# Second expert rows and the choices of the last tiles, set on other picks of one instruction order

## The chip, the cores and the metric

The kernel runs on one core of one Trainium2 chip. The metric is the device time of one execution in microseconds (us); three executions of the kernel before were timed, and a further one was profiled.

## The reference

One step of a decoder layer for 1024 prompt tokens and 64 sample tokens, all in float32, width 1024. The last part, an expert layer, is what the change is about:

```python
h = x + mixed @ w_out                        # mixed: gated pooling mixer and attention
q = (hn @ w_query).reshape(C, 8, 2, 128)     # hn = rmsnorm(h)
s = einsum('chpd,hpnd->chpn', q, sub_keys)   # 8 heads, two halves, 128 sub-keys each
s1, i1 = top_k(s[:, :, 0], 16); s2, i2 = top_k(s[:, :, 1], 16)
idx = the 16 best of the 16 x 16 sums, as i1 * 128 + i2
a = gelu(einsum('cd,chkd->chk', hn, peer_u[idx]))
out = h + einsum('chk,chkd->cd', softmax(top) * a, peer_v[idx])
```

So each token takes 8 x 16 = 128 rows of `peer_u` (a first row, for a dot product) and the same 128 rows of `peer_v` (a second row, for a weighted sum). Each table has 16384 rows of 4 KB.

## The kernel before, in words

**Tiles and groups.** Tokens lie in nine tiles of 128 (tile 4 has the 64 sample tokens). Three groups of tiles, [0, 1], [2, 3, 4] and [5 to 8], go one after the other through the dense part: projections (PE, L1339), pooling, attention, gates (L1585 and L1603), output and query projections (L1631). `lay_out(g)` sets the steps of a group in slots, and `choose(t)` those of a choice, which is the top-k of one tile on DVE (`top_a`, `top_b`, `fin_a`, `fin_b`, L2316 to L2385). The first tile of each group has its choice inside `lay_out`.

**Picks.** A pick n gathers one first row for each of 128 tokens: one indirect DMA of POOL's queue (L975) moves 128 rows of 4 KB, 512 KB, into `ubuf`, and DVE makes the dots (L2401). There are 1088 picks, tile after tile. For all tiles but 3 and 5 a second row is gathered too (L987, also 512 KB, into `vbuf`), 832 in all. It is weighted and added either on DVE (L2422, into `acc`) or on PE as a product with a diagonal matrix (L1717, two matmuls into `pY`, with the matrix made on ACT, L1997). Both buffers are rings of eight.

**Dense pass.** The second rows of tiles 3 and 5 are not gathered. Between picks 712 and 1086 the whole of `peer_v` streams through (128 transfers of 512 KB on SP's queue), DVE builds one-hot matrices (L2459 and L2462), PE turns them into weight matrices (L1674) and multiplies (L1690). During picks 708 to 774 and 904 to 959 the dots read their second operand in PSUM (`pb`) instead of SBUF (`hnf`).

**The order.** Every engine runs one fixed list. `program` goes over the picks n, and behind each pick's own work come the slots that are due at n:

```python
for n in range(NPK + LAG + 5):
    picks(n)
    for slot in DUE.get(n, ()):
        run_slot(stages, slot)
```

`spread(slots, n0, n1)` puts a group's or a choice's slots on the picks from n0 to n1, in proportion to estimated weights. `GROUP_AT` and `CHOOSE_AT` hold these n0 and n1. `TAKEN[n // 32]` says how many second rows are taken in each stretch of 32 picks, and `OWN` how many of these DVE weighs itself; the rest are PE's. A loop makes `VAT` from it (which second rows at which pick), at most two at a pick and not before pick m + 6 for row m. So these tables set the place of POOL's issues and of DVE's and PE's weighing in their lists.

Of the kernel before, what the change touches and what calls it, by code (L numbers as in the profile page):

```python
# [22 lines left out]
def build(nc, x_prompt, x_sample, cache_k, cache_v, cache_logf, state_pool, page_table, norm_mix_g, w_in,  # L23
# [135 lines left out]
    def tile_of(n):  # L159
        return [t for t in range(NT + 1) if START[t] <= n < ENDS[t]][0]  # L160
# [286 lines left out]
    def choose(t):  # L447


        slots = [[("q_load", (t, 0)), ("q_load", (t, 1))], [(x, (t, 0)) for x in CHOICE[0]]]  # L450
        for e in range(PH):
            slots.append([("top_a", (t, e))])
            if e % 2 and e + 1 < PH:
                slots[-1].append(("q_load", (t, e + 1)))
            slots.append([("top_b", (t, e))])
            if e + 1 < PH:
                slots[-1] += [(x, (t, e + 1)) for x in CHOICE[0]]
            if e % 2:
                if e + 2 < PH:
                    slots[-1].append(("q_load", (t, e + 2)))  # L460
                slots.append([("fin_a", (t, e - 1, 2)), ("gexp", (t, e - 1)), ("gexp", (t, e))])
                slots.append([("fin_b", (t, e - 1, 2))])
        return slots
# [85 lines left out]
    def spread(slots, n0, n1):  # L549
        weights = []  # L550
        for slot in slots:
            pe = sum(cost(*x)[0] for x in slot)
            dve = sum(cost(*x)[1] for x in slot)
            weights.append(0.6 + max(pe + 0.6, dve + 0.8))
        total, run = sum(weights), 0.0
        for slot, wt in zip(slots, weights):
            DUE.setdefault(n0 + int((n1 - n0) * run / total), []).append(slot)
            run += wt

    GROUP_AT = [(0, 53), (50, 280), (281, 597)]  # L560
    CHOOSE_AT = {1: (52, 108), 3: (282, 364), 4: (410, 492), 6: (602, 690), 7: (730, 824), 8: (852, 940)}
    ALONE = []
    for g in range(GN):
        slots, ready = lay_out(g)
        if g == 0:
            ALONE = slots[:ready]
            spread(slots[ready:], 0, GROUP_AT[0][1])
        else:
            spread(slots, *GROUP_AT[g])
    for t in CHOOSE_AT:  # L570
        spread(choose(t), *CHOOSE_AT[t])
    for ps in range(len(PASSES)):
# [35 lines left out]

    NI, WIN = 4, 32
    NV = len(VPICK)  # L610
    TAKEN = [18, 15, 15, 14, 10, 8, 10, 12, 34, 30, 32, 35, 29, 27, 33, 17, 21, 19, 32, 16, 16, 4, 18, 37, 32, 32, 32, 40, 26, 34, 36, 28, 30, 32, 8]
    OWN = [0, 0, 3, 9, 10, 8, 10, 10, 4, 15, 16, 7, 28, 16, 19, 15, 20, 13, 9, 0, 0, 1, 2, 0, 6, 16, 23, 7, 0, 0, 10, 8, 13, 15, 3]
    assert sum(TAKEN) >= NV
    last_slot = {}
    for t in GATHERED:
# [8 lines left out]
    for n in range(NPK + LAG):  # L624
        target += TAKEN[n // WIN] / WIN
        while v < NV and len(VAT.get(n, [])) < 2 and VPICK[v] + LAG <= n and (v + 0.5 < target or latest[v] <= n):
            k = VPICK[v] - START[tile_of(VPICK[v])]
            owed += OWN[n // WIN] / max(1, TAKEN[n // WIN])
            on_dve = k < 4 or (k > 4 and owed >= 0.5)
# [1899 lines left out]
```

## Time and profile before

| | |
|---|---|
| median of 3 executions | 3563.71 us (3558.7 to 3564.55) |
| the profiled execution, its own time | 3595.53 us |
| its span | 3593.7 us, 32980 instructions |
| busy, share of the span | PE 86%, DVE 73%, POOL 63%, ACT 26% |
| DMA | 1261.64 MB, of which 1006.76 MB by POOL's gathers |

The first pick's gather is issued at 286 us. The page's busy times don't add up to the span, because the engines work side by side; a stage is read by its stretch. The views by stretch used here have the cuts at the start of the gather of every 32nd pick, so each answers to one number of `TAKEN`.

### The profile page before, as it was taken

Reading aid. Unit: us, or ns where it says so; the run is one execution under the profiler, and the core shown is the slowest. Engines: PE = TensorE matmul, PEld = TensorE weight load, DVE = VectorE, ACT = ScalarE, POOL = GpSimd, SP = SyncE. Lnnn points to the kernel's source line nnn. Section 1 sums busy time; section 2 is a strip of 40 time slices with the busy share of each in tenths; the row PEclk is TensorE's granted clock in tenths of the full one; section 3 lists DMA queues with packets and bytes.
Section 4 is the critical chain, followed back from the end, with each engine's and each line's share of the span. In section 5 each row is a group of like instructions: output and inputs, shape, how many; then the busy total and the mean of one; then the engine's idle time right before and its main releaser. Section 6 shows DMA issues by size and latency. Waiting matters only on the chain.

```text
span 3593.7 us, 32980 instructions
## 1 busy us (share of the span) xinstructions
PE 3075.8 (86%) x9090; PEld 1560.4 (43%) x9090; DVE 2613.4 (73%) x6266; ACT 936.7 (26%) x2287; POOL 2260.8 (63%) x1942
## 2 busy tenths in 40 slices
PE   7897697899987998978998896539998899999987
PEld 4665344467654443333443431115543344544433
DVE  2217877797678888777888898878976768864555
ACT  2112232432123331153331221115510014520000
POOL 0006643577557666878886677776677766677774
PEclk9898898767998998988998998769999899999999
DMA  6359986899999999998999999999999999999999
GB/s 153 99 157 371 363 286 219 284 379 370 372 336 383 370 388 330 329 369 315 383 385 406 400 398 379 357 371 348 351 409 409 409 408 409 369 372 409 409 409 378
DMA packets 426300, 1261.64 MB, mean 351 GB/s; under 512 B 61063, under 2 KB 106791, under 8 KB 426106
## 3 DMA queue, kind: packets, MB, share of 16 engines
q0 software_dynamic: 276480, 1006.76, 73.3%
q1 hardware_dynamic: 141701, 247.01, 20.3%
q10 hardware_dynamic: 7936, 5.77, 0.5%
q8 instruction: 74, 1.21, 0.1%
q14 instruction: 109, 0.89, 0.1%
HBM read 1230.09 MB, written 29.29 MB: 350 GB/s over the span
## 4 chain that ended last, share of the span: by engine, by line
PE 48%; DMA 15%; POOL 12%; DVE 11%; issue 9%; ACT 3%; another core or an unknown queue 2%; SPq 0%; ACTq 0%; DVEq 0%; POOLq 0%
PE pY L1717 13%; DMA vbuf<-in_peer_v_dram,idx 8%; PE pb L1585 8%; POOL ubuf L975 7%; PE pb L1690 5%; POOL vbuf L987 5%; PE pb L1339 4%; DVE ubuf L2401 4%; PE pb L1674 3%; PE pb L1603 3%; PE pb L1631 2%; DMA ubuf<-in_peer_u_dram,idx 2%; DVE acc L2422 1%; PE pb L1442 1%
## 5 line engine op out<-in xcount | busy, mean ns | idle before, releaser
L975 POOL DMA_INDIRECT ubuf<-in_peer_u_dram,idx x1088 | 1275.8, 1173 | 902.2 <-issue 301.4
L2401 DVE CUSTOM_DVE_ANT_0 ubuf<-ubuf,hnf 128x1024 f32<-128x1024 f32 x967 | 1168.6, 1221 | 316.1 <-DMA ubuf<-in_peer_u_dram,idx 292.5
L1717 PE MATMUL pY<-vbuf,dg 128*128 128x512 f32 (+1 forms) x2064 | 1058.7, 644 | 279.3 <-DMA vbuf<-in_peer_v_dram,idx 139.4
L987 POOL DMA_INDIRECT vbuf<-in_peer_v_dram,idx x832 | 981.9, 1180 | 413.2 <-issue 234.9
L1717 PEld LDWEIGHTS pY<-vbuf,dg 128*128 128x128 f32 (+1 forms) x2064 | 376.5, 195 | 772.0 <-issue 539.1
L1690 PE MATMUL pb<-R 128*128 128x512 f32 x1024 | 461.9, 596 | 0.0
L2422 DVE SCALAR_TENSOR_TENSOR acc<-vbuf,gw,acc 128x1024 f32<-128x1024 f32 x316 | 405.4, 1283 | 58.7 <-DMA vbuf<-in_peer_v_dram,idx 46.9
L1585 PE MATMUL pb<-R 128*128 128x256 f32 (+2 forms) x1152 | 361.1, 474 | 5.0 <-DMA R<-in_w_in_dram 3.8
L1987 ACT ACTIVATE gel<-dots 128x4 f32<-128x4 f32 x272 | 55.4, 204 | 1023.9 <-DVE dots L2401 842.0
L1690 PEld LDWEIGHTS pb<-R 128*128 128x128 f32 x1024 | 195.7, 192 | 245.4 <-issue 245.4
L1585 PEld LDWEIGHTS pb<-R 128*128 128x128 f32 x1152 | 221.7, 193 | 142.0 <-issue 94.8
L1997 ACT ACTIVATE dg<-ident,gw 128x128 f32<-128x128 f32 (+1 forms) x516 | 189.4, 384 | 350.3 <-DVE gw L2408 251.7
L1631 PE MATMUL pb<-R 128*128 128x256 f32 (+2 forms) x768 | 249.5, 480 | 5.5 <-DMA R<-in_w_query_dram 4.7
L1339 PE MATMUL pb<-R 128*128 128x512 f32 (+1 forms) x432 | 195.3, 600 | 9.4 <-DVE R L2042 9.4
L1631 PEld LDWEIGHTS pb<-R 128*128 128x128 f32 x768 | 148.1, 196 | 97.2 <-issue 68.2
L1674 PEld LDWEIGHTS pb<-R 128*128 128x128 f32 x1024 | 130.9, 194 | 97.4 <-ACT R L1958 50.7
L1674 PE MATMUL pb<-R 128*128 128x64 f32 x1024 | 136.9, 278 | 25.1 <-ACT R L1958 21.8
L2401 DVE CUSTOM_DVE_ANT_0 ubuf<-ubuf,pb 128x1024 f32<-128x1024 f32 x121 | 146.7, 1213 | 8.1 <-DMA ubuf<-in_peer_u_dram,idx 6.7
L1603 PE MATMUL pb<-R 128*128 128x512 f32 (+1 forms) x288 | 129.3, 610 | 10.4 <-DVE R L2285 10.4
L1987 ACT ACT_TABLE_LOAD x107 | 137.3, 1283 | 2.5 <-issue 0.5
L1958 ACT ACTIVATE R<-R 128x64 f32<-128x64 f32 x512 | 134.6, 336 | 10.3 <-DVE R L2462 7.5
L1339 PEld LDWEIGHTS pb<-R 128*128 128x128 f32 (+1 forms) x432 | 78.3, 186 | 105.7 <-issue 95.5
(260 smaller groups left out, 2749.7 us busy)
## 6 DMA issues: line engine op xcount, KB each, us to landing
R<-in_peer_v_dram SPq DMA_DIRECT2D x128, 512.0 KB
R<-in_w_in_dram SPq DMA_DIRECT2D x12, 2048.0 KB
R<-in_w_in_dram SPq DMA_DIRECT2D x24, 1024.0 KB
R<-in_w_query_dram SPq DMA_DIRECT2D x24, 1024.0 KB
ubuf<-in_peer_u_dram,idx POOLq DMA_INDIRECT x1088
vbuf<-in_peer_v_dram,idx POOLq DMA_INDIRECT x832
R<-in_w_out_dram SPq DMA_DIRECT2D x12, 1024.0 KB
R<-in_x_prompt_dram SPq DMA_DIRECT2D x16, 512.0 KB, 9.0
```

What stands on the lines that cost most here:

```text
L975: pool.indirect_dma_start(out=ubuf[:, n % RING, :], out_offset=None, in_=peer_u[0], in_offset=bass.IndirectOffsetOnAxis(ap=idx[:, t % NI, ...
L987: pool.indirect_dma_start(out=vbuf[:, v % RING, :], out_offset=None, in_=peer_v[0], in_offset=bass.IndirectOffsetOnAxis(ap=idx[:, t % NI, ...
L1339: ins = pe.matmul(pb[0:rows, 2 + o % 3, :], xnT(g)[:, c, cols(i)], wr[j % 2][:, c, :], start=(c == 0), stop=(c == KD - 1))
L1585: ins = pe.matmul(pb[:, out % 5, 0:N], w_four(x)[:, d % NG, kk * P:(kk + 1) * P], rhs, start=(d == 0), stop=(d == last))
L1603: ins = pe.matmul(pb[0:rows, b0 + half, :], mixedT(g)[:, c, cols(i)], w_rows(12 + c // 2)[:, c % 2, half * 512:(half + 1) * 512], start=(c ...
L1631: ins = pe.matmul(pb[:, 2 * (e % 2) + c, 0:N_[g]], w_cols(x)[:, d, c * P:(c + 1) * P], hnT(g)[:, d, :], start=(d == 0), stop=(d == KD - 1))
L1674: ins = pe.matmul(pb[:, 4, c:c + NB], oh_a[o % OHR][:, a, :], oh_b[o % OHR][:, a, :], start=True, stop=True)
L1690: ins = pe.matmul(pb[:, 2 * j + c, :], dw[j][:, b % NB, :], vr[u % VRR][:, c * 512:(c + 1) * 512], start=(b % NB == 0), stop=(b % NB == NB ...
L1717: ins = pe.matmul(pY[0:rows, half, :], dg[:, CPE[m] % RDG, 0:rows], vbuf[:, v % RING, half * 512:(half + 1) * 512], start=first, stop=(t ! ...
L1987: act.activation(gel[:, q % 2, :], dots[:, q % 2, :], ACT.Gelu).then_inc(gel_d, 1)
L2401: dve.tensor_tensor_reduce(ubuf[:, n % RING, :], ubuf[:, n % RING, :], hn, 1.0, 0.0, ALU.mult, ALU.add, dots[:, q % 2, n % GRP:n % GRP + 1 ...
L2422: dve.scalar_tensor_tensor(a, vbuf[:, v % RING, :], gw[:, t % NI, k:k + 1], a, ALU.mult, ALU.add).then_inc(v_dve, 1)
```

## The change

Only four tables of numbers change:

```diff
--- before.py
+++ after.py
@@ -557,8 +557,8 @@
             DUE.setdefault(n0 + int((n1 - n0) * run / total), []).append(slot)
             run += wt
 
-    GROUP_AT = [(0, 53), (50, 280), (281, 597)]
-    CHOOSE_AT = {1: (52, 108), 3: (282, 364), 4: (410, 492), 6: (602, 690), 7: (730, 824), 8: (852, 940)}
+    GROUP_AT = [(0, 50), (50, 280), (281, 600)]
+    CHOOSE_AT = {1: (52, 108), 3: (282, 364), 4: (416, 492), 6: (602, 690), 7: (718, 836), 8: (840, 940)}
     ALONE = []
     for g in range(GN):
         slots, ready = lay_out(g)
@@ -608,8 +608,8 @@
 
     NI, WIN = 4, 32
     NV = len(VPICK)
-    TAKEN = [18, 15, 15, 14, 10, 8, 10, 12, 34, 30, 32, 35, 29, 27, 33, 17, 21, 19, 32, 16, 16, 4, 18, 37, 32, 32, 32, 40, 26, 34, 36, 28, 30, 32, 8]
-    OWN = [0, 0, 3, 9, 10, 8, 10, 10, 4, 15, 16, 7, 28, 16, 19, 15, 20, 13, 9, 0, 0, 1, 2, 0, 6, 16, 23, 7, 0, 0, 10, 8, 13, 15, 3]
+    TAKEN = [18, 15, 15, 14, 14, 4, 22, 8, 34, 30, 42, 33, 21, 35, 29, 13, 13, 19, 28, 16, 16, 8, 18, 37, 22, 32, 32, 50, 26, 30, 36, 28, 30, 24, 20]
+    OWN = [0, 0, 3, 9, 14, 4, 22, 6, 4, 15, 21, 7, 21, 20, 18, 13, 13, 15, 8, 0, 0, 2, 2, 0, 4, 16, 23, 8, 0, 0, 10, 8, 13, 8, 7]
     assert sum(TAKEN) >= NV
     last_slot = {}
     for t in GATHERED:
```

As the loop lays them out, the second rows by stretch are (all others stay as they are, and so do those from pick 704 on, except that single rows there move between DVE and PE):

| picks | before: rows (DVE + PE) | now |
|---|---|---|
| 128 to 160 | 10 (10 + 0) | 14 (14 + 0) |
| 160 to 192 | 8 (8 + 0) | 4 (4 + 0) |
| 192 to 224 | 10 (10 + 0) | 22 (22 + 0) |
| 224 to 256 | 12 (10 + 2) | 8 (6 + 2) |
| 320 to 352 | 32 (16 + 16) | 42 (21 + 21) |
| 352 to 384 | 35 (7 + 28) | 33 (7 + 26) |
| 384 to 416 | 29 (27 + 2) | 21 (20 + 1) |
| 416 to 448 | 27 (17 + 10) | 35 (21 + 14) |
| 448 to 480 | 33 (19 + 14) | 29 (18 + 11) |
| 480 to 512 | 17 (15 + 2) | 13 (13 + 0) |
| 512 to 544 | 21 (20 + 1) | 13 (13 + 0) |
| 544 to 576 | 19 (13 + 6) | 19 (15 + 4) |
| 576 to 608 | 32 (9 + 23) | 28 (8 + 20) |
| 672 to 704 | 4 (1 + 3) | 8 (2 + 6) |

Up to pick 384 that is 249 rows, was 233; from 384 to 640 it is 174, was 194. In all 832 remain, 313 of them on DVE (was 316). Group 0's rest now ends at pick 50 (was 53) and group 2 at 600 (was 597). Tile 4's choice lies on picks 416 to 492 (was 410 to 492), tile 7's on 718 to 836 (was 730 to 824), tile 8's on 840 to 940 (was 852 to 940).

**DVE at picks 204 and 205**, inside the gates of group 1 (L2283 and L2285 are merges of the gates, L2408 the weights of four picks). Before:

```order
L2401 ISA ubuf,dots<-ubuf,hnf 128x1024
L2401 ISA dots 128x1
L2283 TENSOR_TENSOR R<-R,pb 128x320
L2285 TENSOR_TENSOR R<-R 128x320
L2401 ISA ubuf,dots<-ubuf,hnf 128x1024
L2401 ISA dots 128x1
L2408 TENSOR_TENSOR gw<-gel,gw 128x4
L2283 TENSOR_TENSOR R<-R,pb 128x320
L2285 TENSOR_TENSOR R<-R 128x320
L2283 TENSOR_TENSOR R<-R,pb 128x320
L2285 TENSOR_TENSOR R<-R 128x320
```

Now:

```order
L2401 ISA ubuf,dots<-ubuf,hnf 128x1024
L2401 ISA dots 128x1
L2422 SCALAR_TENSOR_TENSOR acc<-vbuf,gw,acc 128x1024
L2283 TENSOR_TENSOR R<-R,pb 128x320
L2285 TENSOR_TENSOR R<-R 128x320
L2401 ISA ubuf,dots<-ubuf,hnf 128x1024
L2401 ISA dots 128x1
L2408 TENSOR_TENSOR gw<-gel,gw 128x4
L2422 SCALAR_TENSOR_TENSOR acc<-vbuf,gw,acc 128x1024
L2283 TENSOR_TENSOR R<-R,pb 128x320
L2285 TENSOR_TENSOR R<-R 128x320
L2283 TENSOR_TENSOR R<-R,pb 128x320
```

Behind the dot of pick 204, and again behind that of pick 205, now stands a second row on DVE (L2422), ahead of the merges.

**DVE at picks 393 to 397**, in group 2's attention. Before:

```order
L2422 SCALAR_TENSOR_TENSOR acc<-vbuf,gw,acc 128x1024
L2401 ISA ubuf,dots<-ubuf,hnf 128x1024
L2401 ISA dots 128x1
L2422 SCALAR_TENSOR_TENSOR acc<-vbuf,gw,acc 128x1024
L2401 ISA ubuf,dots<-ubuf,hnf 128x1024
L2401 ISA dots 128x1
L2422 SCALAR_TENSOR_TENSOR acc<-vbuf,gw,acc 128x1024
L2401 ISA ubuf,dots<-ubuf,hnf 128x1024
L2401 ISA dots 128x1
L2422 SCALAR_TENSOR_TENSOR acc<-vbuf,gw,acc 128x1024
L2401 ISA ubuf,dots<-ubuf,hnf 128x1024
L2401 ISA dots 128x1
```

Now:

```order
L2422 SCALAR_TENSOR_TENSOR acc<-vbuf,gw,acc 128x1024
L2401 ISA ubuf,dots<-ubuf,hnf 128x1024
L2401 ISA dots 128x1
L2401 ISA ubuf,dots<-ubuf,hnf 128x1024
L2401 ISA dots 128x1
L2422 SCALAR_TENSOR_TENSOR acc<-vbuf,gw,acc 128x1024
L2434 TENSOR_TENSOR acc<-pY,acc 128x1024
L2401 ISA ubuf,dots<-ubuf,hnf 128x1024
L2401 ISA dots 128x1
L2422 SCALAR_TENSOR_TENSOR acc<-vbuf,gw,acc 128x1024
L2401 ISA ubuf,dots<-ubuf,hnf 128x1024
L2401 ISA dots 128x1
```

Before, a dot and a second row take turns; now some dots have no second row behind them, and the end of tile 1 (L2434, an addition that reads PSUM) comes between.

**Runs of DVE.** A run is here an unbroken row, in DVE's list, of operations that read two full rows in SBUF: dots on `hnf` and second rows (L2422), with at most the small L2408 between them. Operations of runs beyond their third number 52 before and 58 now on picks 128 to 256, 118 and 97 on picks 384 to 512, 27 and 36 on picks 512 to 544.

**DVE at picks 742 and 743**, among the one-hot matrices of the dense pass (L2459, L2462). Before:

```order
L2401 ISA ubuf,dots<-ubuf,pb 128x1024
L2401 ISA dots 128x1
L2459 TENSOR_TENSOR R<-iota,R 128x512
L2462 TENSOR_TENSOR R<-iota,R 128x256
L2401 ISA ubuf,dots<-ubuf,pb 128x1024
L2401 ISA dots 128x1
L2335 TENSOR_TENSOR eq<-v 128x64
L2335 TENSOR_TENSOR eq<-v 128x48
L2339 MAX top_s<-eq 128x8
L2340 MAX_INDEX top_p<-top_s,eq 128x8
```

Now:

```order
L2401 ISA ubuf,dots<-ubuf,pb 128x1024
L2401 ISA dots 128x1
L2459 TENSOR_TENSOR R<-iota,R 128x512
L2462 TENSOR_TENSOR R<-iota,R 128x256
L2401 ISA ubuf,dots<-ubuf,pb 128x1024
L2401 ISA dots 128x1
L2459 TENSOR_TENSOR R<-iota,R 128x512
L2462 TENSOR_TENSOR R<-iota,R 128x256
```

Tile 7's choice had a step here (L2335 to L2343, its `top_b`); on its longer stretch no step is due at pick 743.

## Rows read from the trace of the kernel before

**Rows 1.** The page: busy time of each engine; DMA in 40 slices, in tenths.

```profile
PE 3075.8 (86%) x9090; PEld 1560.4 (43%) x9090; DVE 2613.4 (73%) x6266; ACT 936.7 (26%) x2287; POOL 2260.8 (63%) x1942
...
DMA  6359986899999999998999999999999999999999
```

**Rows 2.** Busy time by stretches of 32 picks, a late one: us, engines, PEclk, DMA share, GB/s.

```profile
3254.70:3352.20 97.50, 97.50 (x228) 42.94 (x227) 48.56 (x75) 8.10 (x27) 69.26 (x65) 1.00 1.03 409
```

**Rows 3.** The same view, picks 384 to 544 and 576 to 608.

```profile
1493.60:1590.50 96.90, 75.56 (x189) 29.20 (x188) 76.55 (x109) 40.25 (x64) 78.29 (x62) 0.88 0.95 343
1590.50:1701.70 111.20, 87.37 (x219) 35.85 (x218) 85.39 (x212) 44.85 (x81) 90.09 (x60) 0.83 0.90 326
1701.70:1805.30 103.60, 101.38 (x241) 44.60 (x241) 87.92 (x199) 31.16 (x55) 83.78 (x66) 1.00 1.02 381
1805.30:1882.20 76.90, 76.90 (x183) 34.02 (x182) 67.86 (x137) 26.62 (x37) 61.98 (x49) 1.00 1.00 381
1882.20:1972.60 90.40, 72.92 (x169) 33.27 (x168) 72.84 (x111) 16.39 (x29) 60.27 (x54) 0.87 1.02 406
...
2067.60:2167.20 99.60, 90.15 (x217) 35.40 (x216) 95.92 (x305) 27.99 (x62) 72.52 (x64) 0.97 1.03 395
```

**Rows 4.** Instructions of POOL between 1493 and 1883 us, grouped by line.

```profile
L975 POOL DMA_INDIRECT ubuf<-in_peer_u_dram,idx x129 | 174.9, 1356 | 42.5 <-issue 39.0 <-DVE dots L2401 3.4
L987 POOL DMA_INDIRECT vbuf<-in_peer_v_dram,idx x107 | 141.8, 1325 | 32.6 <-issue 31.7 <-PE pY L1717 0.9
```

**Rows 5.** Timeline of POOL, then of DVE, at the longest gather issue.

```profile
1505.89 10.48 POOL L987 DMA_INDIRECT vbuf<-in_peer_v_dram,idx  x1 [0.30 <-issue]
1516.67 0.93 POOL L975 DMA_INDIRECT ubuf<-in_peer_u_dram,idx  x1 [0.31 <-issue]
...
1514.34 1.21 DVE L2401 CUSTOM_DVE_ANT_0 ubuf<-ubuf,hnf 128x1024 f32<-128x1024 f32 x1
```

**Rows 6.** Busy time by stretches of 32 picks: picks 128 to 256, then 320 to 384.

```profile
692.00:778.90 86.90, 79.42 (x382) 51.99 (x379) 79.12 (x161) 27.66 (x48) 60.15 (x43) 0.76 1.01 378
778.90:857.10 78.20, 76.13 (x337) 58.11 (x337) 67.03 (x138) 17.91 (x31) 65.42 (x40) 0.63 1.00 371
857.10:942.70 85.60, 83.38 (x303) 57.97 (x303) 53.60 (x92) 23.57 (x33) 51.27 (x43) 0.98 1.01 370
942.70:1055.10 112.40, 100.26 (x310) 56.70 (x309) 76.71 (x159) 23.58 (x44) 55.58 (x45) 0.94 0.95 355
...
1266.50:1377.50 111.00, 105.54 (x264) 45.52 (x263) 94.07 (x223) 35.09 (x71) 73.12 (x65) 0.98 1.00 368
1377.50:1493.60 116.10, 99.68 (x261) 45.82 (x261) 98.10 (x214) 14.59 (x47) 80.45 (x68) 0.90 0.99 345
```

**Rows 7.** The page: dots and second rows, on DVE and on PE.

```profile
L2401 DVE CUSTOM_DVE_ANT_0 ubuf<-ubuf,hnf 128x1024 f32<-128x1024 f32 x967 | 1168.6, 1221 | 316.1 <-DMA ubuf<-in_peer_u_dram,idx 292.5
...
L1717 PE MATMUL pY<-vbuf,dg 128*128 128x512 f32 (+1 forms) x2064 | 1058.7, 644 | 279.3 <-DMA vbuf<-in_peer_v_dram,idx 139.4
...
L2422 DVE SCALAR_TENSOR_TENSOR acc<-vbuf,gw,acc 128x1024 f32<-128x1024 f32 x316 | 405.4, 1283 | 58.7 <-DMA vbuf<-in_peer_v_dram,idx 46.9
```

**Rows 8.** Busy time by stretches of 32 picks: picks 672 to 704, then 736 to 768.

```profile
2307.60:2361.80 54.20, 13.07 (x20) 3.35 (x20) 51.39 (x132) 5.81 (x18) 40.01 (x36) 0.59 0.94 346
...
2449.60:2547.50 97.90, 88.39 (x405) 53.81 (x404) 86.04 (x230) 56.41 (x199) 64.74 (x65) 1.00 0.96 351
```

**Rows 9.** Instructions of DVE between 2449 and 2548 us, by line.

```profile
L2401 DVE CUSTOM_DVE_ANT_0 ubuf<-ubuf,pb 128x1024 f32<-128x1024 f32 x32 | 38.8, 1212 | 0.0
L2459 DVE TENSOR_TENSOR R<-iota,R 128x512 f32<-128x512 f32 x34 | 23.3, 686 | 5.9 <-PE pb L1674 2.7 <-remote 2.4 <-issue 0.6
L2462 DVE TENSOR_TENSOR R<-iota,R 128x256 f32<-128x256 f32 x34 | 14.4, 423 | 0.0
```

**Rows 10.** Waits of POOL, then of DVE, between 857 and 943 us.

```profile
POOL ubuf L975 <- DVE dots L2401: 22.4, 7, 6.7
...
DVE R L2281 <- PE pb L1585: 16.1, 7, 7.0
```

## Prediction of the time after the change

> **What bounds the kernel now.** The page first: no engine is busy throughout, PE has 86% of the span, DVE 73%, POOL 63%, but the DMA line stands at 9 from the seventh slice nearly to the end [rows 1]. So I went on to the busy times by stretches of 32 picks. A late one shows what a full DMA looks like: share 1.03 at 409 GB/s [rows 2]. A gathered row of 512 KB, 524288 bytes, then costs 1.28 us. I take 1.03 as full, and for a stretch of T us call T x (1.03 - share) / 1.03 its DMA room.
>
> The second thing to see is in the stretches from pick 384 to 512 [rows 3]. The share falls to 0.95 and 0.90, yet PE and DVE are not full. POOL is: between 1493 and 1883 us its 129 + 107 = 236 gathers take 174.9 + 141.8 = 316.7 us, and 42.5 + 32.6 = 75.1 us lie between them, 0.3 us of issue each but for about 4 us [rows 4]. Together that is the whole stage. A plain issue takes 0.93 us and 0.31 us before it [rows 5], so 1.24 us per row, close to the DMA's own 1.28. Over 0.94 us each, the 236 issues spend 316.7 - 221.8 = 94.9 us too much. The worst takes 10.48 us, and through it DVE runs dots and second rows without a pause; the last of these is a dot from 1514.34 us on, and it is 0.8 us after that dot's end that POOL is through [rows 5]. I read it as POOL held up by DVE's runs.
>
> A rule of the Trainium skill speaks on this, "SBUF — State Buffer", section Who interferes with whom: a DVE instruction with two SBUF inputs contends only with a GpSimd instruction that reads SBUF, and a lock lasts for one instruction. By that alone a gather would lose one dot's time at most, and the trace doesn't agree: 10.48 us is eight of them.
>
> **The change, part by part.** Nothing is added or removed but a place: 832 second rows before and after. What a row costs is what bounds its new place, and what it gives is what bounded its old one.
>
> *Rows added, picks 128 to 384* (16 more) [rows 6]. On picks 128 to 160, 4 more: 5.1 us of DMA, less room of 86.9 x 0.02 / 1.03 = 1.7, is +3.4. On 160 to 192, 4 fewer, but PE is busy 76.1 of 78.2 us and the rows are DVE's, so only 2.1 of 5.1 us comes out: -2.1. On 192 to 224, 12 more, all weighed on DVE: 15.4 less room of 1.7 is +13.7. DVE carries it: 53.6 + 12 x 1.283 [rows 7] = 69.0 us in a stretch that is then 99.3. On 224 to 256, 4 fewer where share is 0.95 and something else leads (at its best 5.1): I take -2.0, nearer nothing, since PE is busy 100.3 of 112.4. On 320 to 352, 10 more: 12.8 less room of 3.2 is +9.6; PE's 105.5 gets 5 rows of two matmuls of 0.644 us [rows 7], 112.0, which is below the new 120.6. On 352 to 384, 2 fewer, PE's: -1.3, half of what DMA or PE would give. Sum: +21.3. Bounds: the 26 added rows at the full 1.28 and nothing given back by the 10 removed, +33; the added ones as here and the removed ones at 1.28, 3.4 + 13.7 + 9.6 - 12.8 = +13.9.
>
> *Rows removed, picks 384 to 640* (20 fewer) [rows 3]. On 384 to 416, 8 fewer issues of 1.24 give -9.9, and on 416 to 448, 8 more take them back, +9.9, since POOL leads in both. On 448 to 480, 4 fewer: -5.0. On 480 to 512, 4 fewer, but PE is busy all of the 76.9 us and loses 2 rows, 2.6 us; between 2.6 and 5.0 I take -4.0. On 512 to 544, 8 fewer with the DMA at 1.02: -10.3. On 576 to 608, 4 fewer, where DVE is at 95.9 of 99.6 and gets rid of a single row, 1.3 us: between 1.3 and 5.1 I take -3.2. Sum: -22.5. Bounds: all 20 rows at 1.28, -26; where PE, DVE or half a row's price decides (3.9 and 2.6 by PE's rows, 5, 1.3), -13.
>
> *The four rows on picks 672 to 704* find DMA room of 54.2 x 0.09 / 1.03 = 4.7 for their 5.1 us, PE nearly idle, and DVE at 51.4 of 54.2, which takes one row more [rows 8]. +1.0, bounds 0 and +5.
>
> *POOL's long issues.* 97 operations stand beyond the third of DVE's runs on picks 384 to 512, was 118, and 133 instead of 145 with the next stretch: 8% to 18% fewer. Of the 94.9 us [rows 4] that would be 8 to 17 us; but many issues are a little long in every stage, and the later start of tile 4's choice packs DVE tighter from pick 416 on. I take -5, bounds +5 and -15. (By the skill's rule, named above, this term is 0 and the sum 5 us less of a gain.)
>
> *Longer choices of tiles 7 and 8.* On picks 736 to 768 DVE is busy 86.0 us of 97.9, and waits most of the rest; the DMA has room for 97.9 x 0.07 / 1.03 = 6.7 us [rows 8]. Of the 86.0, dots are 38.8 and one-hot matrices 23.3 + 14.4 [rows 9]; some 8 us are left for the choice, and at 118 picks instead of 94 a fifth of that goes, 1.7 us. Tile 8's brings about as much or less further on. Together -3, bounds 0 and -8 (room of 6.7 and a bit). Work brought forward to picks 718 to 730 meets a DVE with time to spare. The ends of groups 0 and 2, moved by 3 picks, and single rows that change between DVE and PE after pick 704, where the DMA leads [rows 2], I cost at nothing: at 409 GB/s the transfers hide them; were that cover gone, three rows at 1.283 us are 4 us at most.
>
> **Sum.** 21.3 - 22.5 + 1.0 - 5.0 - 3.0 = -8.2 us. The profiled execution took 3595.5 us, so it would be 3587.3; the median of the timed ones is 3563.7, 0.9% lower, and I carry the difference over as it is: **3555.5 us**.
>
> **The rivals.**
> 1. *A mere exchange.* If POOL's long issues stay as they are and the later stages don't move, then rows cost what they save: 21.3 - 22.5 + 1.0 = -0.2, and with half of the choices' gain -1.7, so 3562 us. For it: row prices of 1.24 and 1.28 are nearly one. Against it: the 94.9 us. It is also where the skill's rule leads. Chance 0.22.
> 2. *The long issues mostly go.* They need a full run of DVE, and the alternation of dot and second row on picks 384 to 416 is what the plan thins out most (27 to 20 on DVE). If 20 of the 94.9 us go in place of 5, it ends at -23, 3540 us. Against it: 21 of the rows of the next stretch are DVE's, was 17. Chance 0.17.
> 3. *PE's clock falls under the gates.* This is the one on the slow side. On picks 192 to 224 PE works 83.4 of 85.6 us at a granted clock of 0.98, and DVE waits 16.1 us for its gates [rows 6, 10]. With 12 more rows the stretch gets 99.3 us long, PE waits for merges that DVE does after a late dot, and a PE with gaps has had 0.76 and 0.63 just ahead, 0.83 to 0.88 on picks 384 to 448 [rows 3, 6]. At 0.98 x 83.4 / 99.3 = 0.82 it becomes the bound; at 0.75 the stretch takes 109 us, +10, and picks 320 to 352 (PE 112 of 120.6) get the same, some +5. With POOL's relief gone besides, which the added runs on picks 192 to 224 can undo, it's -8.2 + 10 + 5 + 3 = +10, so 3574 us. Against it: PE's gates are fed by four buffers ahead, and POOL waits 22.4 us for dots there [rows 10], so it is not short of time. Chance 0.21.
>
> That the plan doesn't do what it says is no rival: the loop's counts are in the table above, and all gathers keep their distance of six picks.
>
> **The numbers.** The forecast has 0.40, its own range is -2 to -15 (all bounds at once would be -35 to +30, which is not likely, since the terms are apart). A measurement of this kernel can tell some 0.2%, 7 us, from no change, so of the 0.40 I put 0.28 on faster and 0.12 on the same. Rival 1: 0.03 faster, 0.17 the same, 0.02 slower. Rival 2: all 0.17 faster. Rival 3: 0.02 the same, 0.19 slower. Sum: 0.48, 0.31, 0.21. The range reaches from 3532, rival 2 and a stronger relief, to 3577, rival 3 and a little more.
>
> **What would show it.** Picks 128 to 384 should take 21 us longer (801.6 us before, from 692.0 to 1493.6), picks 384 to 640 some 27 us less (740.9 before, 1493.6 to 2234.5), picks 736 to 768 between 1 and 6 less. The clock on picks 192 to 224 should stay above 0.9; below 0.82, rival 3 is right. POOL's issues on picks 384 to 512 should have fewer above 3 us; as many as before speak for rival 1. The forecast is wrong if the first part grows by more than 30 us, or if the stages after pick 704, which I count at -3, move by more than 8 either way.

## The result and the profile after

| | before | the change |
|---|---|---|
| median of 7 executions | 3564.18 us | 3532.89 us |
| ratio, 95% interval | | 0.9918 [0.9898, 0.9939] |
| profiled execution, its span | 3593.7 us | 3525.3 us |

The change makes the kernel 0.8% faster, 31 us of the medians. The forecast was 3555.5, that is 8 us faster, so the gain is nearly four times what was forecast; the result is at the lower edge of the range, 0.9 us inside it. The two profiled executions differ by 68 us, over twice that. Picks 704 to 960 alone account for 28 us of it (793.3 and 765.7 us), and the experiments show that these are no part of the change.

The page's lines that answer to [rows 1]:

```profile
PE 3075.5 (87%) x9102; PEld 1566.2 (44%) x9102; DVE 2608.8 (74%) x6263; ACT 931.3 (26%) x2285; POOL 2245.0 (64%) x1942
...
DMA  6349986799999999999999999999999999999999
```

The busy times hardly move (PE 3075.5, DVE 2608.8, POOL 2245.0 us): the work is the same, and what goes is idle time.

Busy time by stretches of 32 picks, in the columns of [rows 2], for picks 128 to 256 and 320 to 384, as in [rows 6]:

```profile
687.40:775.30 87.90, 81.56 (x370) 55.48 (x369) 82.79 (x163) 27.00 (x46) 66.42 (x47) 0.73 1.04 397
775.30:851.60 76.30, 75.20 (x348) 57.81 (x346) 62.21 (x132) 19.62 (x33) 54.81 (x36) 0.66 0.99 356
851.60:941.80 90.20, 85.47 (x304) 59.15 (x305) 66.03 (x107) 23.57 (x33) 64.90 (x55) 0.96 1.03 401
941.80:1053.50 111.70, 100.44 (x308) 56.19 (x307) 74.27 (x155) 23.63 (x44) 50.90 (x40) 0.94 0.95 355
...
1257.90:1390.40 132.50, 120.41 (x301) 52.26 (x299) 108.82 (x249) 37.59 (x77) 83.44 (x74) 0.97 0.99 368
1390.40:1490.00 99.60, 91.27 (x240) 42.19 (x241) 89.39 (x191) 13.25 (x42) 79.77 (x66) 0.95 1.03 375
```

Picks 192 to 224 grew from 85.6 to 90.2 us with 12 rows more, at 401 GB/s, was 370, and PE's clock was 0.96, before 0.98. Picks 320 to 352 took 132.5 us, was 111.0, but the next 32 took 99.6, was 116.1. The cuts lie at POOL's issues, and POOL moves against the others, so these two are read together: 232.1 us, was 227.1, with 8 rows more.

The same view for picks 384 to 544, as in [rows 3]:

```profile
1490.00:1575.80 85.80, 68.47 (x187) 27.97 (x186) 63.47 (x101) 38.59 (x63) 69.64 (x54) 0.90 0.97 351
1575.80:1685.10 109.30, 88.97 (x221) 36.19 (x220) 91.70 (x209) 45.68 (x83) 88.88 (x67) 0.86 0.98 354
1685.10:1781.30 96.20, 94.84 (x229) 41.73 (x228) 84.09 (x200) 31.01 (x53) 77.57 (x62) 1.00 1.03 396
1781.30:1857.00 75.70, 75.70 (x180) 33.52 (x179) 71.48 (x148) 21.13 (x32) 57.81 (x46) 1.00 0.99 374
1857.00:1934.70 77.70, 69.27 (x163) 31.52 (x162) 64.94 (x103) 13.65 (x28) 53.35 (x46) 0.93 1.02 406
```

Together 444.7 us, was 479.0. POOL's gathers on picks 384 to 512, to be held against [rows 4]:

```profile
L975 POOL DMA_INDIRECT ubuf<-in_peer_u_dram,idx x129 | 172.1, 1334 | 43.5 <-issue 38.1 <-DVE dots L2401 5.4
L987 POOL DMA_INDIRECT vbuf<-in_peer_v_dram,idx x98 | 122.8, 1253 | 29.9 <-issue 29.6 <-PE pY L1717 0.3
```

There are 227 issues in 367 us; over 0.94 us each they spend 294.9 - 213.4 = 81.5 us, was 94.9 for 236. Issues of over 3 us on picks 384 to 512 number 9 now and 8 before.

### The profile page after: what moved, and what is told of

Read it like the earlier page. It is cut to its first block, busy times and chain, and to the rows that moved or that the text cites. A ratio compares the mean times of both kernels' runs of the same rounds, so it can differ in the third digit from the quotient of the medians.

```text
span 3525.3 us, 32998 instructions
## 1 busy us (share of the span) xinstructions
PE 3075.5 (87%) x9102; PEld 1566.2 (44%) x9102; DVE 2608.8 (74%) x6263; ACT 931.3 (26%) x2285; POOL 2245.0 (64%) x1942
## 4 chain that ended last, share of the span: by engine, by line
PE 46%; DMA 15%; POOL 11%; DVE 9%; issue 6%; SPq 2%; ACT 2%; ACTq 0%; DVEq 0%; POOLq 0%
PE pY L1717 15%; DMA vbuf<-in_peer_v_dram,idx 8%; POOL ubuf L975 7%; PE pb L1690 7%; PE pb L1585 6%; POOL vbuf L987 5%; PE pb L1339 3%; PE pb L1603 3%; DVE ubuf L2401 3%; PE pb L1674 3%; PE pb L1631 2%; DMA ubuf<-in_peer_u_dram,idx 2%; PE pb L1442 1%; PE pb L1558 1%; DVE acc L2422 1%
## 5 line engine op out<-in xcount | busy, mean ns | idle before, releaser
L1717 PE MATMUL pY<-vbuf,dg 128*128 128x512 f32 (+1 forms) x2076 | 1058.1, 641 | 226.5 <-DMA vbuf<-in_peer_v_dram,idx 152.4
L987 POOL DMA_INDIRECT vbuf<-in_peer_v_dram,idx x832 | 964.2, 1159 | 390.4 <-issue 202.2
L1717 PEld LDWEIGHTS pY<-vbuf,dg 128*128 128x128 f32 (+1 forms) x2076 | 379.4, 195 | 719.9 <-issue 470.5
L2422 DVE SCALAR_TENSOR_TENSOR acc<-vbuf,gw,acc 128x1024 f32<-128x1024 f32 x313 | 401.8, 1284 | 45.2 <-DMA vbuf<-in_peer_v_dram,idx 41.3
L1987 ACT ACTIVATE gel<-dots 128x4 f32<-128x4 f32 x272 | 55.4, 204 | 988.3 <-DVE dots L2401 987.1
L1339 PE MATMUL pb<-R 128*128 128x512 f32 (+1 forms) x432 | 195.7, 599 | 11.1 <-DVE R L2042 11.1
```

What stands on the lines that cost most here:

```text
L987: pool.indirect_dma_start(out=vbuf[:, v % RING, :], out_offset=None, in_=peer_v[0], in_offset=bass.IndirectOffsetOnAxis(ap=idx[:, t % NI, ...
L1339: ins = pe.matmul(pb[0:rows, 2 + o % 3, :], xnT(g)[:, c, cols(i)], wr[j % 2][:, c, :], start=(c == 0), stop=(c == KD - 1))
L1717: ins = pe.matmul(pY[0:rows, half, :], dg[:, CPE[m] % RDG, 0:rows], vbuf[:, v % RING, half * 512:(half + 1) * 512], start=first, stop=(t ! ...
L1987: act.activation(gel[:, q % 2, :], dots[:, q % 2, :], ACT.Gelu).then_inc(gel_d, 1)
L2422: dve.scalar_tensor_tensor(a, vbuf[:, v % RING, :], gw[:, t % NI, k:k + 1], a, ALU.mult, ALU.add).then_inc(v_dve, 1)
```

## Experiments

There are three sets of four kernels, each set on a chip of its own with the kernel before beside it; ratios are against it on the same chip. The time of a stretch of picks is that of one profiled execution. In the diffs, OWN goes with TAKEN as in the change, unless it is shown.

**The kernel before once more, profiled.** No edit.

> The kernel before, unchanged, profiled once more, to see how far a stretch of 32 picks moves from one profiled execution to the next. The first profile took 3595.5 us where the timed executions took 3564. Theory A (the gain lies in picks 384 to 640): the stretches from pick 704 to 960 come out near 766 us here too, as in the profile of the change, not 793 as in the first profile, so that the 28 us lost there are of that one execution. Theory B (the later stages really gained from the longer choices): 793 us again, within 5. Time between 3555 and 3600 us.

Measured: 3616.4 us on a chip where the kernel before has a median of 3646 in 23 executions. Picks 704 to 960 took 805 us. Neither A's 766 nor B's 793 came out, nor a time between 3555 and 3600, so this chip alone doesn't decide it; the last set does. This one execution is 30 us faster than the median, which is to be kept in mind where its stretches are compared below.

**The plan alone.**

```diff
-    TAKEN = [18, 15, 15, 14, 10, 8, 10, 12, ...
+    TAKEN = [18, 15, 15, 14, 14, 4, 22, 8, ...
-    OWN = [0, 0, 3, 9, 10, 8, 10, 10, ...
+    OWN = [0, 0, 3, 9, 14, 4, 22, 6, ...
```

> The change's TAKEN and OWN alone; the ranges of groups and choices as before. Theory A (the plan of second rows carries the gain): ratio 0.992 to 0.995, some 18 to 30 us faster. Theory B (the choices of tiles 7 and 8 carry it): ratio 0.998 to 1.001. Theory C (half and half): about 0.996. My prediction's terms without those of the choices give -5 us, ratio 0.9985.

Measured: 0.9897 [0.9864, 0.9931]. The plan carries the gain (A, and somewhat beyond it). The stretches 320 to 384, 384 to 448 and 448 to 512 of the kernel before, on that chip:

```profile
1266.30:1496.40 230.10, 206.64 (x524) 91.92 (x523) 192.40 (x436) 49.63 (x118) 153.65 (x131) 0.93 0.98 351
1496.40:1702.50 206.10, 160.08 (x410) 64.56 (x409) 161.88 (x320) 84.71 (x145) 169.49 (x120) 0.86 0.94 338
1702.50:1886.70 184.20, 178.74 (x423) 78.65 (x422) 158.52 (x340) 59.98 (x94) 149.42 (x115) 1.00 1.00 377
```

and with the plan alone:

```profile
1279.10:1502.80 223.70, 209.71 (x533) 92.64 (x532) 196.53 (x440) 49.52 (x117) 157.70 (x140) 0.95 1.03 376
1502.80:1708.80 206.00, 158.80 (x411) 64.21 (x409) 156.12 (x314) 83.68 (x146) 165.78 (x120) 0.88 0.92 332
1708.80:1879.40 170.60, 168.82 (x401) 74.21 (x401) 155.44 (x342) 58.53 (x91) 131.71 (x106) 1.00 1.02 393
```

With 8 rows more, picks 320 to 384 became 6.4 us shorter, at 376 GB/s. With 8 fewer, picks 448 to 512 became 13.6 us shorter. On picks 384 to 448 the number of rows is the same (8 fewer, then 8 more), and so is the time. The whole profiles differ by 9.5 us only (3614.6 and 3605.1), the medians by 39: that of the kernel before was a fast execution.

**The choices of tiles 7 and 8 alone.**

```diff
-    CHOOSE_AT = {... 7: (730, 824), 8: (852, 940)}
+    CHOOSE_AT = {... 7: (718, 836), 8: (840, 940)}
```

> Only the choices of tiles 7 and 8 get their longer ranges (718 to 836 and 840 to 940). Theory A: ratio 0.998 to 1.0 (my term was -3 us, 0.9992). Theory B: 0.992 to 0.995, and picks 704 to 960 are over 15 us shorter in the profile, with the DMA share above 1.0 on picks 736 to 768, was 0.96. Theory C: about 0.996.

Measured: 0.9986 [0.9962, 1.0009], as A had it; the interval holds both my -3 us and nothing. Picks 704 to 960 took 805.5 us, against 805.1 of the kernel before.

**The other ranges alone.**

```diff
-    GROUP_AT = [(0, 53), (50, 280), (281, 597)]
+    GROUP_AT = [(0, 50), (50, 280), (281, 600)]
-    CHOOSE_AT = {... 4: (410, 492) ...}
+    CHOOSE_AT = {... 4: (416, 492) ...}
```

> Only the ends of group 0 (50) and group 2 (600), the start of group 2's and tile 4's choice as in the change (tile 4 on 416 to 492). I costed these at nothing: ratio 0.999 to 1.001. A rival: tile 4's choice, packed tighter, costs up to 5 us by itself (1.0014), or its later start frees POOL on picks 410 to 416 and gains up to 5 (0.9986).

Measured: 0.9959 [0.9934, 0.9984], faster by more than either side expected; nothing was not right. In its profile POOL's excess over 0.94 us on picks 384 to 448 is 42 us, against 56 to 57 in the two profiles of the kernel before, and on picks 448 to 512 it is 44, was 39 and 42. The stretch 384 to 448 took 202.2 us, was 208.1 and 206.1, but the next one, to 512, took 188.1 us, was 180.5 and 184.2, so the two together are as long as before: the profiles don't show where the time of this run was gained.

**The change whole, in the second set.** No edit to the change.

> The change whole, on the chip of this set. If its parts add up as on the last chip (0.9897 x 0.9986 x 0.9959), the ratio is 0.984; if it repeats its own first comparison, 0.992. The stretch from pick 704 to 960 is 766 us in the first profile of the change and 793 to 809 us in all others: if that belongs to the change, it is again under 780 here; if to the chip or to the one execution, it is within 8 us of the other kernels of this set.

Measured: 0.9946 [0.9914, 0.9978]. The parts do not add up to 0.984. Picks 704 to 960 took 811.8 us, as the others of the set (807 to 818), so the short 766 is not the change's.

**The early part of the plan alone.**

```diff
 TAKEN, of the stretches of 32 picks from 128, and of the one from 512:
-10, 8, 10, 12 ... 21
+14, 4, 22, 8 ... 13
```

> The plan changed only on picks 128 to 256 (8 rows more in sum) and 512 to 544 (8 fewer). By my prediction's prices, DMA room taken from the busy share: +13.0 - 10.3 = +3 us, ratio 1.001. Theory R (the room is what is missing to 409 GB/s, some 8 us on picks 192 to 224, so the 8 rows come in for 3 us or less): +3 - 10.3 = -7 us, ratio 0.998, with picks 128 to 256 between 0 and 5 us longer (363 and 358 us before) and picks 512 to 576 some 10 us shorter (185 and 182 us).

Measured: 1.0022 [0.9988, 1.0057]. The time can't tell the two: R's 0.998 is just outside, my ledger's 1.001 well inside. Picks 512 to 576 took 173.5 us, 8 to 12 shorter, as both had it; picks 128 to 256 took 365.5 us, 2 to 8 longer than in the profiles of the kernel before on other chips. On this set's own chip they took 369.4 us in the middle part alone, which has no row added there, so here the 8 rows cost nothing that shows. Part of the time is picks 384 to 448, 218.7 us and thus 10 longer without an edit there; one other profile has that too. Picks 192 to 224 in it, with 22 rows, at 398 GB/s and a clock of 0.98:

```profile
865.50:954.90 89.40, 84.15 (x305) 58.45 (x306) 65.96 (x106) 23.57 (x33) 63.95 (x55) 0.98 1.03 398
```

**The middle part alone.**

```diff
 TAKEN, of the six stretches of 32 picks from 320 on:
-32, 35, 29, 27, 33, 17
+42, 33, 21, 35, 29, 13
```

> The plan changed only on picks 320 to 512: 10 more and 2 fewer up to 384, 8 fewer and 8 more up to 448, 8 fewer up to 512. By my prediction's prices +8.3 - 9.0, and -5 for POOL's long issues: -6 us, ratio 0.998. Theory R (room up to 409 GB/s): +0.4 - 9.0 - 5 = -14 us, ratio 0.996. If the long issues of POOL are no matter: 5 us less gain in both, and the excess of POOL's issues over 0.94 us on picks 384 to 512 stays at 92 us or more.

Measured: 0.9951 [0.9926, 0.9976], -18 us, between -9 and -27. My -6 is outside, R's -14 inside. POOL's excess on picks 384 to 512 stayed at 57 + 35 = 92 us, so its long issues had no part in this, and R's number without them is -9, at the edge of the interval. So the middle part is the greater half of the gain. Picks 320 to 384 with their 8 added rows took 224.4 us, against 228.1 in the early part alone on the same chip, so my +8.3 for them was off.

**Twelve rows more on picks 192 to 224.**

```diff
 the change, and of TAKEN (from 192; from 448 and 480):
-22 ... 29, 13
+34 ... 23, 7
 OWN: 34 ... 15, 7
```

> The change and 12 rows more on picks 192 to 224 (34, all weighed on DVE), taken from picks 448 to 512 (6 and 6). Theory R: the room there is used up by the change's own 12 (share 1.03 at 401 GB/s), so these cost 15 us and bring 15 us: no different from the change, within 4 us. If rows come in free there still (PE or DVE's waits for gates lead): 10 to 15 us faster than the change. If PE's clock falls below 0.82 there, as my slow rival had it: slower than the change by 5 us or more.

Measured: 0.9955 [0.9928, 0.9982], beside 0.9946 of the change: no difference, as R had it, and as 1.28 us a row at either end would have it. The stretch took 104.9 us and PE kept its clock:

```profile
860.60:965.50 104.90, 99.20 (x353) 68.53 (x354) 80.19 (x117) 26.06 (x37) 79.84 (x66) 0.97 1.03 396
```

Picks 128 to 256 grew by 16.6 us against the change on this chip (369.8), picks 448 to 512 shrank by 9.3 (175.9 to 166.6). The slow rival, the clock under the gates, is out: 0.97 with PE at 99.2 of 104.9 us.

**The change and the plan alone, once more, in the third set.**

> The change whole once more, beside the three kernels below on one chip: ratio 0.992 to 0.995, as its first two comparisons (0.9918 and 0.9946).

> TAKEN and OWN alone, a second time (0.9897 on another chip). If the ranges of groups and choices give nothing on top of the plan: the same as the change whole, within 0.003. If they give what they gave alone (0.9959 x 0.9986): 0.005 above the change. Picks 384 to 512 should show POOL's excess over 0.94 us at 53 + 32 us, as in the first profile of this kernel, against 40 to 46 + 36 to 44 us with the new ranges.

Measured: 0.9930 [0.9903, 0.9956] and 0.9946 [0.9927, 0.9965]. On top of the plan the ranges and choices give 0.0016, within the intervals, and less than the 0.0055 that they gave alone. POOL's excess with the plan alone was 54 + 29 us, as expected; with the change 49 + 35, so its first part was not quite down to 46. Picks 736 to 768 of the change here:

```profile
2415.50:2502.00 86.50, 85.32 (x395) 52.41 (x394) 82.08 (x210) 53.47 (x190) 64.62 (x65) 1.00 1.03 408
```

of the plan alone, with the old choices:

```profile
2420.30:2509.20 88.90, 84.74 (x385) 52.38 (x383) 81.20 (x221) 54.28 (x192) 65.58 (x65) 0.98 1.02 401
```

and of the change on the second set's chip:

```profile
2447.30:2550.90 103.60, 94.11 (x407) 57.28 (x406) 86.67 (x221) 56.56 (x201) 66.94 (x64) 0.94 0.93 334
```

The longer choices make 2.4 us here, close to my term. On the first set's chip the same picks took 97.8, 103.1 and 96.8 us with the old choices and 103.0 with the longer ones, so one profile can't carry it. The chip makes 17 us: the share is 1.03 at 408 GB/s on one and 0.93 at 334 on the other, for the same kernel. Picks 704 to 960 took 763 to 765 us in all four kernels of this set, old choices or new.

**Ten rows more on picks 352 to 384.**

```diff
 the change, and of TAKEN (from 352; from 448 and 480):
-33 ... 29, 13
+43 ... 24, 8
```

> The change and 10 rows more on picks 352 to 384 (43), taken from picks 448 to 512 (5 and 5). In the profiles with 8 more rows on picks 320 to 384 these took 228 us, and 230 us without, so the rows came in free. Theory R (free as long as there is room up to 409 GB/s; on picks 352 to 384 of the change's profile 375 GB/s over 99.6 us, room 8.3 us): the 10 rows cost 4 to 5 us and bring 12, so 7 us faster than the change. Theory F (full, as I priced them): 12.8 us for 12, no difference. Theory P (PE leads there, 91 of 100 us, and 7 of these rows are its own, 9 us): slightly slower or equal.

Measured: 0.9976 [0.9957, 0.9996], slower than the change by 0.0046, some 16 us. Picks 320 to 384 and 448 to 512:

```profile
1258.50:1506.10 247.60, 226.34 (x582) 101.56 (x581) 201.32 (x442) 54.85 (x130) 172.68 (x150) 0.96 0.99 367
1712.60:1880.10 167.50, 161.81 (x381) 71.25 (x380) 147.26 (x340) 49.76 (x81) 126.49 (x97) 0.98 1.00 370
```

and of the change on this chip:

```profile
1260.70:1498.10 237.40, 213.28 (x541) 94.79 (x540) 198.25 (x439) 50.73 (x119) 164.25 (x140) 0.94 0.99 362
1696.40:1867.90 171.50, 170.17 (x406) 75.02 (x405) 158.28 (x355) 51.49 (x85) 134.62 (x106) 1.00 1.01 387
```

R's 7 us faster is out, and F's no difference hardly fits; P (PE leads on the new place) had the direction. The ten rows cost 10.2 us on their new place and gave back 4.0 on the old one; picks 384 to 448 between them, without an edit, took 8.2 us longer (206.5, was 198.3). The old place gives no more: PE is busy 170.2 of 171.5 us there in the change already, and 8 of the 10 rows taken out are DVE's. On the new place all ten rows are PE's, and its busy time grew by 13.0 us. The DMA moved 362 GB/s there, which by R's room up to 409 would have taken them in for nothing.

**PE weighs more on picks 384 to 448.**

```diff
 the change, and of OWN (from 384 and 416):
-21, 20
+11, 12
```

> The change, but on picks 384 to 448 DVE weighs 23 of the 56 second rows instead of 41 and PE the 18 others; operations beyond the third of DVE's runs fall there from 65 to 49. Theory A (DVE's runs hold up POOL's issues): POOL's excess on these picks falls from 40 to 46 us to 30 or less, and the stretch from 195 to 206 us to 185 to 195. Theory B (the skill's rule, or anything else makes the long issues): the excess stays at 40 us or more, the stretch is as long or up to 10 us longer, since PE gets 23 us of work more. Theory A is not told apart from B by the time alone, since PE may lead; the excess tells it.

Measured: 1.0004 [0.9987, 1.0021], slower than the change by 26 us. POOL's excess on these picks fell from 49.0 to 35.1 us; in the other profiles with the change's rows there it is 40 to 46. That is the direction of A, but not its number (30 or less), and the stretch got longer by 20 us. It and DVE's longest wait:

```profile
1492.50:1710.90 218.40, 178.89 (x462) 74.62 (x460) 127.36 (x269) 89.70 (x163) 147.71 (x120) 0.91 0.89 320
...
DVE gw L2408 <- ACT gel L1987: 62.5, 12, 13.3
```

In the change:

```profile
1498.10:1696.40 198.30, 158.80 (x406) 64.23 (x404) 153.56 (x300) 84.26 (x146) 161.70 (x120) 0.87 0.98 346
...
DVE gw L2408 <- ACT gel L1987: 20.6, 7, 10.7
```

POOL's lateness went down, but DVE's waits for the gelu on ACT (L1987) went from 20.6 to 62.5 us. ACT makes the diagonal matrices for each row that PE weighs, in one list with the gelu and attention's exponentials. So fewer rows on DVE go with shorter issues of POOL, though a DVE that waits more may do that as well as one with shorter runs; and giving the rows up costs more than it brings. That ACT's list is the way of this loss is read from the waits; no run tested it by itself.

## Why the prediction was right, and where its sizes were wrong

The direction and the place of the gain were right. The range held by 0.9 us only, at its end for a stronger relief of POOL, which is not what happened, so that it held is in part luck; the forecast's ratio, 0.9977, is outside the interval in two of the three comparisons of the change and at the edge of the third. The sizes of the terms, against the stretches of picks in nine profiles, each side by its mean: without the plan (the kernel before twice, and the two kernels with choices or ranges alone) and with it (the change three times, the plan alone twice):

| picks | without | with | difference | predicted |
|---|---|---|---|---|
| 128 to 256 | 359.4 | 365.7 | +6.2 | +13.0 |
| 256 to 320 | 210.8 | 208.6 | -2.2 | 0 |
| 320 to 384 | 230.1 | 229.5 | -0.6 | +8.3 |
| 384 to 448 | 209.0 | 202.8 | -6.2 | 0 |
| 448 to 512 | 182.6 | 171.5 | -11.1 | -9.0 |
| 512 to 576 | 183.9 | 173.2 | -10.7 | -10.3 |
| 576 to 640 | 172.0 | 171.8 | -0.2 | -3.2 |
| sum | | | -24.8 | -1.2 (and -5 for long issues) |

The two sides are not from the same chips: three of the four without come from the first set's, where the kernel before has a median of 3646 us, three of the five with from chips where it has 3564 and 3565. On the first set's chip alone, picks 128 to 384 took 797.8 to 801.5 us without the plan and 800.3 with it. The -6.2 on picks 384 to 448 is not the plan's: on the first set's chip 206.1 us became 206.0 with the plan alone, and the short times (195.2 to 202.2, but also 206.2) are those of kernels with the new ranges.

1. **Rows added: the term that failed.** I had +21.3; the stretches say +3.4 (means of 800.4 and 803.8 us for picks 128 to 384, which spread over 4 and 10 us). The step was the DMA room, which I took from the busy share, 1.03 less the share. At share 1.01 and 370 GB/s that leaves 1.7 us on picks 192 to 224. With 12 rows more the same stretch moved 401 GB/s. Had I taken the room as what is missing to 409 GB/s, it is 85.6 x 39 / 409 = 8.2 us there, and 111.0 x 41 / 409 + 116.1 x 64 / 409 = 29 us on picks 320 to 384. Then 15.4 - 8.2 = +7 and about 0 come out, near the +4.7 and -0.6 of the means. The middle part alone (0.9951, and 224.4 us on picks 320 to 384) is the run that speaks most against my price. So the added rows came in nearly free, and the distance of the share from 1.03 was no measure of the DMA's room. That the rate up to 409 GB/s is the right measure is not shown: it was fitted to these stretches, and with ten rows more on picks 352 to 384 it failed: the room there is 237.4 x 47 / 409 = 27 us, the rows should have been free, and they cost 10.2 us. There PE's added work, 13.0 us, is the nearer price.
   PE's own price was misread as well. `L1717` has 2064 records for 516 rows, so four to a row and not two, and a row takes some 2 us of PE (1058.7 / 516), not 1.29. The 5 rows on picks 320 to 352 would have made 105.5 into about 116, still below the 120.6, so no term that was taken hangs on it but the ends of some bounds. And the DMA line of the page stands at 9 from the ninth slice on, not the seventh.
2. **Rows removed** were right in sum: -22.5, measured -22.0 on picks 448 to 640.
3. **Picks 672 to 704**, +1.0: picks 640 to 704 took 127.2 us without and 128.0 with the plan. Right within their spread.
4. **POOL's long issues**, -5. The excess on picks 384 to 512 went from a mean of 92 to 84 us, but the issues of over 3 us did not get fewer: 7 or 8 of them in the four profiles without, 7 to 9 in the five with. By the prediction's own sign that speaks for rival 1. On picks 384 to 448 it is the ranges that lower the excess: 53 to 57 us in all seven profiles with the old ranges of groups and of tile 4's choice, and 40 to 49 in all six with the new ones and DVE's share of the change or of before. I had expected the later start of that choice to work the other way. On picks 448 to 512 it is 44 us with the ranges alone, 32 to 42 with neither, 32 and 29 with the plan alone. Over both stretches the plan alone has 85 and 83 us, the ranges alone 86, neither 87 to 99. So the size was met without the cause that I gave, and the share of this in the time stays open: the ranges gave 15 us alone, with an interval from 6 to 24, and 6 on top of the plan, within noise.
5. **Choices of tiles 7 and 8**, -3: 0.9986 alone, with an interval that holds nothing too, and 2.4 us on picks 736 to 768 of one chip. Not contradicted; more can't be told.
6. **The rivals.** A mere exchange is out, by 0.9897 and 0.9946 for the plan alone: the rows cost less than they save. Its other half, that the long issues stay, came true. The long issues' going is out as the cause, though its time, 3540 us, is nearer than mine: the middle part gained its 18 us with the excess at 92. The clock under the gates is out, by 0.95 to 0.98 on picks 192 to 224 with 22 rows there, and 0.97 with 34. Of the low clocks that it leaned on, 0.76 and 0.63 were no sign of a PE with gaps: PE was busy 79.4 of 86.9 and 76.1 of 78.2 us there.
7. **The sum** against one profiled execution carried no error of its own, but a comparison of the two profiles would: 28 of their 68 us lie on picks 704 to 960, where two chips differ by 48 us (764 and 812 us for the change). By the sign that the prediction set itself, more than 8 us after pick 704, it would be wrong on these two profiles; on one chip these picks take the same time with the change and with the plan alone (764.3 and 765.3 us), so the sign most likely read chips and not the change. The other sign, more than 30 us on picks 128 to 384, did not come: 0.9 us.

The change whole has been compared three times: 0.9918, 0.9946, 0.9930. No kernel beat it on a chip where both ran; of two that go on in its direction, 12 rows more early made no difference and 10 more in the middle were slower.

## What to carry to other kernels

Before pricing a transfer by a DMA that seems full, look at what it moves, not only at how long it is busy: 370 GB/s at share 1.01 had room for more. But a rate below the best is no promise of room: at 362 GB/s ten rows more cost 10.2 us, where they were all PE's. When rows are shifted from one stage to another, both ends need their own bound, and the gain ends at the first stage where another engine takes over, as PE did on picks 448 to 512. And two profiles of one kernel on two chips can differ by more than a change is worth, so a stage's gain is believed from several.

## What was not expected of the hardware

The change itself had another speed in one stage on another chip: picks 736 to 768 took 86.5 us at 408 GB/s on one and 103.6 us at 334 GB/s on another, where the whole kernel took 3539 and 3617 us (medians).

A gather issue of POOL grows from 0.93 us to 7 to 12 us at its longest, in each of the 14 profiles, and through it DVE has no gap of more than 0.03 us: it runs dots and second rows out of SBUF with small operations between them, in four of the profiles also steps of a choice. Each profile has 12 to 17 issues of over 3 us, and all of them lie before pick 490. The rule of the Trainium skill that the prediction named ("SBUF — State Buffer", Who interferes with whom) has a lock that ends with the instruction; an issue of 10.48 us, held through nine dots and second rows, doesn't agree with it.

But a DVE without a pause is not enough for such an issue. In the profile of the kernel before DVE is busy without a gap from 1902.8 to 1919.1 us (picks 517 on) too, with dots and second rows, and POOL gets ten issues through, none over 2 us. The lines of DVE and POOL between 1904 and 1919.1 us:

```profile
L2401 DVE CUSTOM_DVE_ANT_0 ubuf<-ubuf,hnf 128x1024 f32<-128x1024 f32 x8 | 9.8, 1229 | 0.0
L975 POOL DMA_INDIRECT ubuf<-in_peer_u_dram,idx x6 | 8.4, 1402 | 3.5 <-DVE dots L2401 1.9 <-issue 1.5
L2422 DVE SCALAR_TENSOR_TENSOR acc<-vbuf,gw,acc 128x1024 f32<-128x1024 f32 x5 | 6.5, 1292 | 0.0
L987 POOL DMA_INDIRECT vbuf<-in_peer_v_dram,idx x4 | 3.7, 937 | 1.2 <-issue 1.2
```

So what makes some issues long and others not, beside runs of the same operations, stays open, and with it the prediction's reading that DVE's runs are what holds POOL up.
